# Two transformer blocks on one core: the recurrence's gates as three products of rounded parts

## The chip, the cores and the metric

The kernel runs on one core of a Trainium2 chip. A core has a matrix engine (TensorE, PE in the profile, with its weight loads as PEld), three engines for elementwise work (VectorE or DVE, ScalarE or ACT, GpSimd or POOL), a synchronisation engine whose queue starts transfers (SP), an on-chip memory of 128 partitions (SBUF) and an accumulator memory of eight banks (PSUM). The engines run their own instruction streams and wait for one another by semaphores. The metric is the device time of one execution in microseconds, smaller being better.

## The reference

Two transformer blocks follow each other on one sequence of 256 tokens with 1024 features, all in f32. The change concerns one part of the first block, the gated recurrence over 1344 channels:

```python
def rg_lru(x, w_a, b_a, w_x, b_x, lam):
    xb = x.reshape(bsz, s, RNN_BLOCKS, RNN_BLOCK_W)        # 16 blocks of 84 channels
    r = sigmoid(einsum('bsnc,ncd->bsnd', xb, w_a).reshape(bsz, s, D_RNN) + b_a)
    i = sigmoid(einsum('bsnc,ncd->bsnd', xb, w_x).reshape(bsz, s, D_RNN) + b_x)
    log_a = LRU_C * r * log_sigmoid(lam)
    a = exp(log_a)
    u = sqrt(-expm1(2.0 * log_a)) * (i * x)
    # h[t] = a[t] * h[t-1] + u[t]

hr = rg_lru(causal_dwconv(rx, rnn_conv_w, rnn_conv_b), ...)
y_rnn = (hr * gelu(rgate)) @ w_rnn_out
```

Around it stand the input projection, an attention with compressed, selected and windowed branches, the output projections, a gated feed-forward part with a short convolution, and a second block of attention, spatial gating and feed-forward.

## The kernel before

All weights are one stream of chunks, at most 128 x 2048 numbers each, in the order of `CHUNKS` (lines 91 to 131). A product in f32 would cost PE several passes, so a chunk is split into two parts that PE takes in one pass each: ACT copies the chunk from its arrival slot `RAW` into `WH` with rounding (line 629), and DVE writes the rest, raw minus rounded, into `WL` (line 1074). Activations are split in the same way (`AH` and `AL`, `BH` and `BL`, and so on), and a product is the sum of high x high, high x low and low x high (lines 1735, 1736 and 1740 for the projections of the recurrence).

There are two arrival slots in this stage (`NRAW`), and three places for split chunks (`NSLOT`). While PE works on chunk c, ACT and DVE split chunk c + 2. SP starts the load of a chunk when the slot's previous chunk has had its low part taken (line 538).

The recurrence runs in five groups of 2, 3, 2, 2 and 2 tiles of up to 126 channels, interleaved with the chunks of the merge gates ("mg"). In the order of the chunks it goes: `rnn` chunks (a projection for one tile of channels and its output gate), `mg` chunks, and behind each group one small chunk `ri` with the weights of the two gates for the group. What each engine does for chunk c is its "window". For an `rnn` chunk PE projects one tile; ACT evicts it into `XC` with the first convolution tap and into `RGT` (lines 793 and 795); DVE adds the other three taps (line 1298). The `ri` chunk is the only one here that isn't split: its f32 weights are loaded straight into the place of the chunk (`WF`, line 551), when the chunk that was there is done, and PE multiplies them in f32 with `XC` (line 2065). Each tile takes one bank for both gates. A block of 84 channels does not fit whole into the tiles, so one block per group is split over the first two tiles, 42 channels each, and its cross terms are small products with 42 rows and 42 columns (lines 2073 and 2075), one of each pair in the lower half of the array's rows and one in the upper half. The gates share two banks with the neighbouring projections (`mb_bank`, line 1828), so a product waits until the reader of two uses earlier has evicted its bank.

After the gates, ACT evicts them as TR and TI (lines 806 and 807), DVE and ACT form a, u and the scan over several windows (`rg_group` says in which), and ACT and DVE split the result into `AH` and `AL` for the projection `ro` (lines 656 and 1153).

The attention of the first block runs through the same windows as twelve units: PE forms scores (line 1858), DVE the maxima (lines 1095 and 1097), ACT the exponentials with their sums (`unit_exp`, line 650), DVE scales them (line 1112), PE transposes them (line 1869) and multiplies by the values (line 1892). The scores of a unit wait for the exponentials of the unit before (line 1852). ACT's order inside a window is written out by hand (lines 1036 to 1056): split a chunk, the exponentials of a unit, the evictions of the chunk, and the small steps of the window. POOL computes only reciprocal roots for the norms (line 575), and some steps of the second block; in the recurrence it has no work.

Of the kernel before, what the change touches and what calls it, by code (L numbers as in the profile page):

```python
# [33 lines left out]
RP = 126  # L34
# [36 lines left out]
def gate_cols(g):  # L71

    return RG_TILES[g] * RP + HB
# [41 lines left out]


def ffn_order(up, n, down, lag=5):

    out, d = [], 0
    for i in range(n):  # L120
        out.append((up, i, CHUNK, True))
        if i >= 2 * d + lag:
# [13 lines left out]
               max(RNN_NO[i] for i in range(RG_AT[g], RG_AT[g + 1])) + 1 for g in range(NG)]  # L136
SPLIT_NO = [sum(1 for x in CHUNKS[:c] if x[3]) for c in range(NCH)]
# [6 lines left out]
def arrival_slots():  # L144

    last, uses, out = [None] * (NRAW + 3), [0] * (NRAW + 3), {}
    for c, (kind, i, _, is_split) in enumerate(CHUNKS):
        if not is_split:
            continue
        third = kind in ("wo", "up", "dn") or kind == "ro" and i >= 1 or kind == "in2" and i < 3  # L150
        slots = list(range(NRAW)) + [NRAW] * third + [NRAW + 1] * (kind in ("up2", "dn2"))
        slots += [NRAW + 2] * (kind == "kv")
        slot = min(slots, key=lambda n: -1 if last[n] is None else last[n])
        out[c] = (slot, last[slot], uses[slot])
        last[slot] = SPLIT_NO[c]
        uses[slot] += 1
    return out
# [87 lines left out]
def two_block_program(nc, A_w, A_x, A_cols, A_consts, A_g1, A_g2, A_og, A_gln, A_ln1, A_ln2, A_ws, A_out):  # L245
    ctx = ExitStack()
    with ctx:
# [45 lines left out]
        def const(name):  # L293
# [160 lines left out]
        y_mean, y_std, eps_ready, x0_low, y_ln, xt4_done, xt4_hi, xt4_lo, up2_silu, up2_prod = (sem(n) for n in (  # L454
            "y_mean", "y_std", "eps_ready", "x0_low", "y_ln", "xt4_done", "xt4_hi", "xt4_lo", "up2_silu", "up2_prod"))
        up2_hi, up2_lo, z_gain, wt_ready, rnn_in, xw_ready, gate_t_done, x_sq2 = (sem(n) for n in (
            "up2_hi", "up2_lo", "z_gain", "wt_ready", "rnn_in", "xw_ready", "gate_t_done", "x_sq2"))
        half_copied, halves_summed = sem("half_copied"), sem("halves_summed")
# [101 lines left out]
        def _(eng):  # L560
# [32 lines left out]
            power(crs[0:NKV * CP, :], css[0:NKV * CP, :], 1, HD, EPS, kc_rstd)  # L593
            for t in range(NT):
# [18 lines left out]
        def _(eng):  # L613
# [358 lines left out]
            def half_copy(c, n, bank):  # L972

                eng.wait_ge(chunk_done, c + 1)
                if n >= 4:
                    eng.wait_ge(up_conv if n - 4 < N_UP else up2_prod, n - 3 if n - 4 < N_UP else n - 3 - N_UP)
# [23 lines left out]
            def up2_silu_of(i):  # L1000
                eng.wait_ge(halves_summed, N_UP + i + 1)
                if i >= 4:
                    eng.wait_ge(up2_lo, i - 3)
                eng.activation(SG[:, i % 4, :], HLS[:, i % 4, 0, :], ACT.Silu).then_inc(up2_silu, 1)

            def up2_first(i):
                eng.wait_ge(up2_prod, i + 1)
                if i >= NA:
                    eng.wait_ge(chunk_done, AT["dn2", (i - NA) // 2] + 1)
                eng.activation(AH[:, i % NA, :], SG[:, i % 4, :], ACT.Copy).then_inc(up2_hi, 1)  # L1010
# [25 lines left out]
            for c in range(NCH):  # L1036
# [6 lines left out]
                if c == SPLIT_AHEAD:  # L1043
                    split(c + 2)
                u = unit_at(c - W0)
# [14 lines left out]
        def _(eng):  # L1060
# [7 lines left out]
            def split(c):  # L1068

                if c >= NCH or not CHUNKS[c][3]:  # L1070
# [445 lines left out]
            def up2_product(i):  # L1516
                eng.wait_ge(halves_summed, N_UP + i + 1)
                eng.wait_ge(up2_silu, i + 1)
                eng.tensor_tensor(SG[:, i % 4, :], HLS[:, i % 4, 1, :], SG[:, i % 4, :], ALU.mult)\
                   .then_inc(up2_prod, 1)  # L1520

            def up2_second(i):
                eng.wait_ge(up2_hi, i + 1)
                eng.tensor_tensor(AL[:, i % NA, :], SG[:, i % 4, :], f32(AH[:, i % NA, :]), ALU.subtract)\
                   .then_inc(up2_lo, 1)
# [188 lines left out]
        def _(eng):  # L1714
# [15 lines left out]
            def f_tile(out, c, col0, m, H, L, nk=KD, parts=P):  # L1730
# [6 lines left out]
                eng.wait_ge(w_lo, SPLIT_NO[c] + 1)  # L1737
# [5 lines left out]
            def hl_tile(bank, c, col0, HL):  # L1743
# [5 lines left out]
                eng.wait_ge(w_lo, SPLIT_NO[c] + 1)  # L1749
# [36 lines left out]
            def tile1_pass(bank, c, HL, lo_ready):  # L1786
# [3 lines left out]
                eng.wait_ge(w_lo, SPLIT_NO[c] + 1)  # L1790
# [4 lines left out]
            def t_part(out, c, cols, ks, H, L, t, start, stop):  # L1795
# [7 lines left out]
                eng.wait_ge(w_lo, SPLIT_NO[c] + 1)  # L1803
# [195 lines left out]
            def main(c):  # L1999
# [58 lines left out]
                if kind == "ri":  # L2058
                    eng.wait_ge(mb_dve, RNN_THROUGH[i])
                    w = plain(c).rearrange("p (a n) -> p a n", a=2)  # L2060
                    banks = {}
                    for m, t in enumerate(gate_order(i)):
                        banks[t] = mb_bank(MB_NO[c] + m)
                        for which in range(2):
                            last = eng.matmul(PS[0:RP, banks[t], 256 * which:256 * which + 256],  # L2065
                                              w[0:RP, which, RP * t:RP * t + RP], XC[:, i % 2, t, :], start=(which == 0),
                                              stop=(t == 2), skip_group_check=True)
                        if t == 2:
                            last.then_inc(ri_part, 1)
                    for which in range(2):  # L2070
                        cols = slice(256 * which, 256 * which + 256)
                        other = w[:, which, RP * RG_TILES[i]:gate_cols(i)]
                        ins = eng.matmul(PS[64:64 + HB, banks[0], cols], other[0:HB], XC[0:HB, i % 2, 1, :],
                                         start=False, stop=(which == 1), skip_group_check=True)
                        last = eng.matmul(PS[0:HB, banks[1], cols], other[64:64 + HB], XC[64:64 + HB, i % 2, 0, :],
                                          start=False, stop=(which == 1), skip_group_check=True)
                    ins.then_inc(ri_part, 1)
                if kind == "ao":
# [10 lines left out]
                    for ks in parts:  # L2089
# [7 lines left out]
                        eng.wait_ge(w_lo, SPLIT_NO[c] + 1)  # L2097
# [4 lines left out]
                if kind == "ro":  # L2102
# [14 lines left out]
                    eng.wait_ge(w_lo, SPLIT_NO[c] + 1)  # L2117
# [34 lines left out]
                if kind in ("dn", "dn2"):  # L2152
                    first_bank, lo_s, n_all = (2, up_lo, N_UP // 2) if kind == "dn" else (0, up2_lo, N_UP2 // 2)
# [6 lines left out]
                    eng.wait_ge(lo_s, 2 * i + 2)  # L2160
# [4 lines left out]
                    elif i == n_all - 2:  # L2165
# [6 lines left out]
                        eng.wait_ge(lo_s, 2 * i + 3)  # L2172
                        eng.wait_ge(up_hi if kind == "dn" else up2_hi, 2 * i + 4)
# [11 lines left out]
                        eng.wait_ge(w_lo, SPLIT_NO[c + 1] + 1)  # L2185
# [3 lines left out]
                        eng.wait_ge(lo_s, 2 * i + 4)  # L2189
# [331 lines left out]
```

## Time and profile before

| | |
|---|---|
| Median of 3 runs | 812.28 us (812.08 to 812.28) |
| Span of the profiled execution, first to last instruction | 810.6 us |
| PE busy | 799.6 us (99%) |
| DVE busy | 599.4 us (74%) |
| ACT busy | 487.0 us (60%) |
| POOL busy | 27.1 us (3%), 38 instructions |
| Chain that ended last | PE 93%, ACT 3%, DVE 2% |

The span is the time from the first to the last instruction of one profiled execution; the runs' times hold a little more around it. Busy times are sums over instructions. Matmuls are pipelined, so one of them is shown with a longer duration than the distance to the next; distances between starts are what a stream of them costs. The chain follows the last instruction back, at each step to what released it. A wait is shown as idle time in brackets behind the instruction that waited, with the one that released it. A matmul in f32 shows as two passes.

### The profile page before, as it was taken

The page shows a single profiled execution, that of the slowest core. Times are in us where ns is not written, and L with a number is a line of the kernel's source. Part 1 is how long each engine was busy: PE and PEld are TensorE (multiplying, and loading weights), DVE is VectorE, ACT ScalarE, POOL GpSimd, SP SyncE. Part 2 cuts the span into 40 slices and gives each one's busy share as a digit, 9 for nine tenths or more (in the row PEclk, how much of TensorE's full clock was granted, in tenths as well). Part 3 has the DMA queues.
Part 4 walks back from the last instruction along what each step waited for, and adds up shares of the span by engine and source line. Part 5 has one row for each costly group of instructions (what it writes and reads, how often), then busy time and mean ns, then how long its engine had stood idle before and what let it go on. Part 6 is the DMA issues. An engine that isn't in the chain of part 4 may idle for free.

```text
span 810.6 us, 11913 instructions
## 1 busy us (share of the span) xinstructions
PE 799.6 (99%) x4813; PEld 693.2 (86%) x4813; DVE 599.4 (74%) x773; ACT 487.0 (60%) x738; POOL 27.1 (3%) x38
## 2 busy tenths in 40 slices
PE   8999999999999999999999999999999999999996
PEld 7889998888888888988888888888888988888885
DVE  6774698998957986897878778877777665655556
ACT  6555598877757454765666566546755654544552
POOL 1102000000000000000000000020110000000000
PEclk9999999999999999999999999999999999999999
DMA  8446432342434674456455555764453655555441
GB/s 337 164 156 251 170 126 104 118 155 73 151 119 159 229 288 156 156 188 227 160 206 174 201 197 175 256 237 147 146 196 121 211 201 196 174 219 191 161 152 52
DMA packets 22630, 143.79 MB, mean 177 GB/s; under 512 B 2608, under 2 KB 3248, under 8 KB 8240
## 3 DMA queue, kind: packets, MB, share of 16 engines
q1 hardware_dynamic: 20880, 137.72, 48.3%
q10 hardware_dynamic: 1696, 5.31, 1.8%
q8 instruction: 38, 0.62, 0.3%
q14 instruction: 16, 0.13, 0.0%
HBM read 141.97 MB, written 1.05 MB: 176 GB/s over the span
## 4 chain that ended last, share of the span: by engine, by line
PE 93%; ACT 3%; DVE 2%; DMA 1%; issue 1%; DVEq 0%; SPq 0%; ACTq 0%
PE PS L1748 19%; PE PS L1752 10%; PE PS L1801 10%; PE PS L1802 10%; PE PS L1805 10%; PE PS L1735 5%; PE PS L1736 4%; PE PS L1740 4%; PE PS L2115 3%; PE PS L1764 2%; PE PS L2094 2%; PE PS L1858 1%; PE PS L1892 1%; PE PS L2119 1%; PE PS L1869 1%; PE PS L2065 1%
## 5 line engine op out<-in xcount | busy, mean ns | idle before, releaser
L1074 DVE TENSOR_TENSOR WL<-RAW,WH 128x2048 fp32r<-128x2048 f32 (+2 forms) x127 | 285.1, 2247 | 31.1 <-ACT WH L629 31.0
L629 ACT ACTIVATE WH<-RAW 128x2048 fp32r<-128x2048 f32 (+2 forms) x127 | 238.2, 1877 | 47.0 <-PE PS L1805 25.7
L1490 DVE TENSOR_TENSOR HLS<-PS,HLS 128x512 f32<-128x512 f32 x46 | 31.7, 689 | 92.7 <-ACT HLS L977 92.7
L1748 PE MATMUL PS<-CHL,WH 128*128 128x512 f32 x352 | 87.9, 392 | 0.0
L1735 PE MATMUL PS<-BHL,WH 128*126 128x256 f32 (+1 forms) x336 | 83.6, 287 | 0.0
L977 ACT ACTIVATE HLS<-PS 128x512 f32<-128x512 f32 x46 | 27.4, 595 | 90.7 <-PE PS L1752 86.3
L1736 PE MATMUL PS<-BHL,WH 128*126 128x256 f32 (+1 forms) x336 | 81.8, 282 | 0.0
L1748 PE MATMUL PS<-BHL,WH 128*128 128x512 f32 x320 | 79.9, 392 | 0.0
L1748 PEld LDWEIGHTS PS<-CHL,WH 128*128 128x128 f32 x352 | 63.9, 189 | 11.8
L1802 PE MATMUL PS<-WH,AHL 128*128 128x512 f32 x176 | 68.8, 391 | 0.0
L1801 PE MATMUL PS<-WH,AHL 128*128 128x512 f32 x176 | 68.7, 390 | 0.0
L1735 PEld LDWEIGHTS PS<-BHL,WH 128*126 128x126 f32 (+1 forms) x336 | 63.4, 189 | 4.6 <-issue 3.7
L1748 PEld LDWEIGHTS PS<-BHL,WH 128*128 128x128 f32 x320 | 58.1, 189 | 10.7
L1736 PEld LDWEIGHTS PS<-BHL,WH 128*126 128x126 f32 (+1 forms) x336 | 63.5, 189 | 0.0
L1801 PE MATMUL PS<-WH,BHL 128*128 128x512 f32 x160 | 63.2, 395 | 0.0
L1802 PE MATMUL PS<-WH,BHL 128*128 128x512 f32 x160 | 62.3, 390 | 0.0
L1805 PE MATMUL PS<-WL,AHL 128*128 128x512 f32 x176 | 54.4, 390 | 0.0
L1752 PEld LDWEIGHTS PS<-CHL,WL 128*128 128x128 f32 x352 | 48.0, 190 | 3.4
L1752 PE MATMUL PS<-CHL,WL 128*128 128x256 f32 x352 | 49.1, 282 | 0.0
L1740 PE MATMUL PS<-BHL,WL 128*126 128x256 f32 (+1 forms) x336 | 46.7, 281 | 0.0
L1752 PEld LDWEIGHTS PS<-BHL,WL 128*128 128x128 f32 x320 | 43.7, 190 | 3.1
L1501 DVE SCALAR_TENSOR_TENSOR CG<-HLS,CV,CG 128x255 f32<-128x255 f32 (+1 forms) x96 | 44.2, 481 | 1.7
(313 smaller groups left out, 1311.1 us busy)
## 6 DMA issues: line engine op xcount, KB each, us to landing
RAW<-in_w_stream SPq DMA_DIRECT2D x108, 1024.0 KB, 4.8
RAW<-in_w_stream SPq DMA_DIRECT2D x11, 1008.0 KB, 4.9
RAW<-in_w_stream SPq DMA_DIRECT2D x8, 704.0 KB, 4.5
WF<-in_w_stream SPq DMA_DIRECT2D x2, 1024.0 KB, 5.4
LN<-in_ln ACTq DMA_DIRECT2D x2, 1024.0 KB, 5.2
WF<-in_w_stream SPq DMA_DIRECT2D x4, 294.0 KB, 3.6
X<-in_x SPq DMA_DIRECT2D x2, 512.0 KB, 4.2
RAW<-in_w_stream SPq DMA_DIRECT2D x2, 512.0 KB, 6.8
```

The lines of the kernel that those rows point to most:

```text
L629: eng.activation(WH[:, c % NSLOT, 0:CHUNKS[c][2]], raw(c), ACT.Copy).then_inc(w_hi, 1)
L1074: eng.tensor_tensor(WL[:, c % NSLOT, 0:CHUNKS[c][2]], raw(c), f32(WH[:, c % NSLOT, 0:CHUNKS[c][2]]), ALU.subtract).then_inc(w_lo, 1)
L1490: eng.tensor_tensor(HLS[:, n % 4, :, :], PS[:, bank:bank + 2, 0:TOK], HLS[:, n % 4, :, :], ALU.add)\
L1501: ins = eng.scalar_tensor_tensor(o, HLS[:, i % 4, v, 0:TOK - s], col("fw", (2 - s) * 2 * N_UP + f), o, ALU.mult, ALU.add)
L1735: eng.matmul(out, wh, H[0:parts, k, :], start=(k == 0), stop=False)
L1736: eng.matmul(out, wh, L[0:parts, k, :], start=False, stop=False)
L1740: last = eng.matmul(out, wl, H[0:parts, k, :], start=False, stop=(k == nk - 1))
L1748: eng.matmul(PS[:, bank, :], wh, HL[:, k, :, :].rearrange("p a t -> p (a t)"), start=(k == 0), stop=False)
L1752: last = eng.matmul(PS[:, bank, 0:TOK], wl, HL[:, k, 0, :], start=False, stop=(k == KD - 1))
L1801: eng.matmul(out, H[:, k, tile], wh, start=(start and n == 0), stop=False)
L1802: eng.matmul(out, L[:, k, tile], wh, start=False, stop=False)
L1805: last = eng.matmul(out, H[:, k, tile], WL[:, s, lo_:lo_ + cols], start=False, stop=(stop and n == len(ks) - 1))
```

## The change

The gate chunks `ri` become split chunks like the others: they arrive in `RAW`, ACT rounds them into `WH`, and POOL, not DVE, takes the low part into `WL`. The tiles of channels are split too: ACT rounds each tile of `XC` into `AH` after DVE's taps, in the window behind its projection, ahead of the exponentials of that window, and POOL takes the low part into `AL`. PE then computes the gates as three products of rounded parts each. The small products of the split block write 106 output rows (0 to 105) instead of 42 at their own offset, with weights padded by zeros, so a gate chunk grows by 64 columns per gate (from 588 to 716 columns for a group of two tiles, from 840 to 968 for three). Counting of the low parts is divided: `LOW_NO` counts those of DVE, `RG_LOW_NO` those of POOL. The semaphores of the second feed-forward part (`up2_silu`, `up2_prod`, `up2_hi`, `up2_lo`) are replaced by going on counting in those of the first (`up_gelu`, `up_prod`, `up_hi`, `up_lo`), with the same events. Every wait on `w_lo` by `SPLIT_NO[c] + 1` becomes one by `LOW_NO[c] + 1`; these lines are left out below.

```diff
 def gate_cols(g):
-    return RG_TILES[g] * RP + HB
+    return RG_TILES[g] * RP + 64 + HB
...
-        out += [("ri", g, 2 * gate_cols(g), False)]
+        out += [("ri", g, 2 * gate_cols(g), True)]
...
+LOW_NO = [sum(1 for x in CHUNKS[:c] if x[3] and x[0] != "ri") for c in range(NCH)]
+_low_order = []
+for _c in range(NCH):
+    _low_order += [x[:2] for x in CHUNKS[_c + 2:_c + 3] if x[0] == "ri"]
+    _low_order += [x[:2] for x in CHUNKS[max(0, _c - 1):_c] if x[0] == "rnn"]
+RG_LOW_NO = {_k: _n + 1 for _n, _k in enumerate(_low_order)}
...
@@ SP, loads
                     if before is not None:
-                        eng.wait_ge(w_lo, before + 1)
+                        if CHUNKS[before][0] == "ri":
+                            eng.wait_ge(rg_low, RG_LOW_NO[CHUNKS[before][:2]])
+                        else:
+                            eng.wait_ge(w_lo, LOW_NO[before] + 1)
...
@@ POOL, behind the roots of the first block's norms
+            for c in range(NCH):
+                if c + 2 < NCH and CHUNKS[c + 2][0] == "ri":
+                    s, n = (c + 2) % NSLOT, CHUNKS[c + 2][2]
+                    eng.wait_ge(w_hi, SPLIT_NO[c + 2] + 1)
+                    eng.tensor_tensor(WL[:, s, 0:n], raw(c + 2), f32(WH[:, s, 0:n]), ALU.subtract).then_inc(rg_low, 1)
+                if c and CHUNKS[c - 1][0] == "rnn":
+                    i = CHUNKS[c - 1][1]
+                    G, t = RG_OF[i]
+                    eng.wait_ge(xc_hi, RNN_NO[i] + 1)
+                    eng.tensor_tensor(AL[0:RP, i, :], XC[:, G % 2, t, :], f32(AH[0:RP, i, :]), ALU.subtract).then_inc(rg_low, 1)
...
@@ ACT
+            def rg_round(i):
+                G, t = RG_OF[i]
+                eng.wait_ge(mb_dve, RNN_NO[i] + 1)
+                eng.activation(AH[0:RP, i, :], XC[:, G % 2, t, :], ACT.Copy).then_inc(xc_hi, 1)
...
                 if c == SPLIT_AHEAD:
                     split(c + 2)
+                if c and CHUNKS[c - 1][0] == "rnn":
+                    rg_round(CHUNKS[c - 1][1])
                 u = unit_at(c - W0)
                 if u is not None:
                     unit_exp(u)
...
@@ DVE
             def split(c):
-                if c >= NCH or not CHUNKS[c][3]:
+                if c >= NCH or not CHUNKS[c][3] or CHUNKS[c][0] == "ri":
                     return
...
@@ PE
                 if kind == "ri":
-                    eng.wait_ge(mb_dve, RNN_THROUGH[i])
-                    w = plain(c).rearrange("p (a n) -> p a n", a=2)
+                    eng.wait_ge(rg_low, max(RG_LOW_NO["rnn", k] for k in range(RG_AT[i], RG_AT[i + 1])))
+                    wh, wl = (W[:, c % NSLOT, 0:2 * gate_cols(i)].rearrange("p (a n) -> p a n", a=2) for W in (WH, WL))
                     banks = {}
                     for m, t in enumerate(gate_order(i)):
+                        k = RG_AT[i] + t
                         banks[t] = mb_bank(MB_NO[c] + m)
+                        outs = [PS[0:RP, banks[t], 256 * which:256 * which + 256] for which in range(2)]
                         for which in range(2):
-                            last = eng.matmul(PS[0:RP, banks[t], 256 * which:256 * which + 256],
-                                              w[0:RP, which, RP * t:RP * t + RP], XC[:, i % 2, t, :], start=(which == 0),
+                            rows = wh[0:RP, which, RP * t:RP * t + RP]
+                            eng.matmul(outs[which], rows, AH[0:RP, k, :], start=(which == 0), stop=False, skip_group_check=True)
+                            eng.matmul(outs[which], rows, AL[0:RP, k, :], start=False, stop=False, skip_group_check=True)
+                        for which in range(2):
+                            last = eng.matmul(outs[which], wl[0:RP, which, RP * t:RP * t + RP], AH[0:RP, k, :], start=False,
                                               stop=(t == 2), skip_group_check=True)
                         if t == 2:
                             last.then_inc(ri_part, 1)
+                    first = RG_AT[i]
                     for which in range(2):
                         cols = slice(256 * which, 256 * which + 256)
-                        other = w[:, which, RP * RG_TILES[i]:gate_cols(i)]
-                        ins = eng.matmul(PS[64:64 + HB, banks[0], cols], other[0:HB], XC[0:HB, i % 2, 1, :],
-                                         start=False, stop=(which == 1), skip_group_check=True)
-                        last = eng.matmul(PS[0:HB, banks[1], cols], other[64:64 + HB], XC[64:64 + HB, i % 2, 0, :],
-                                          start=False, stop=(which == 1), skip_group_check=True)
+                        for n, (W, A) in enumerate(((wh, AH), (wh, AL), (wl, AH))):
+                            other = W[:, which, RP * RG_TILES[i]:gate_cols(i)]
+                            ins = eng.matmul(PS[0:64 + HB, banks[0], cols], other[0:HB, 0:64 + HB], A[0:HB, first + 1, :],
+                                             start=False, stop=(which == 1 and n == 2), skip_group_check=True)
+                            last = eng.matmul(PS[0:64 + HB, banks[1], cols], other[64:64 + HB, 0:64 + HB], A[64:64 + HB, first, :],
+                                              start=False, stop=(which == 1 and n == 2), skip_group_check=True)
                     ins.then_inc(ri_part, 1)
```

## Rows read from the trace of the kernel before

**Rows 1.** The page: span, busy time of each engine, chain by engine.
```profile
span 810.6 us, 11913 instructions
...
PE 799.6 (99%) x4813; PEld 693.2 (86%) x4813; DVE 599.4 (74%) x773; ACT 487.0 (60%) x738; POOL 27.1 (3%) x38
...
PE 93%; ACT 3%; DVE 2%; DMA 1%; issue 1%; DVEq 0%; SPq 0%; ACTq 0%
```
**Rows 2.** Windows: length, busy PE, PEld, DVE, ACT, POOL, clock, DMA.
```profile
98.80:122.50 23.70, 23.70 (x191) 21.69 (x190) 22.57 (x33) 22.77 (x48) 0.00 (x0) 1.00 0.41 147
...
137.30:152.90 15.60, 15.08 (x126) 13.82 (x126) 14.82 (x18) 14.82 (x36) 0.00 (x0) 1.00 0.52 194
...
200.00:243.00 43.00, 43.00 (x339) 36.29 (x337) 32.44 (x43) 27.62 (x54) 0.00 (x0) 1.00 0.38 130
```
**Rows 3.** Line 2065, the gates' f32 products: passes, duration in ns, shape.
```profile
L2065 PE MATMUL PS<-XC,WF x44: 377/379/482, 98.9 to 240.7; 126*126 126x256 f32 x44
```
**Rows 4.** The chain through the gates of group 2: start, length, engine, line.
```profile
161.83 1.92 PE PS L2065 x8
163.75 0.34 PE PS L2073
...
164.77 1.06 PE PS L1869 x8
```
**Rows 5.** Timeline of PE, a projection in rounded parts: start, length.
```profile
103.01 0.28 PE L1736 MATMUL PS<-BHL,WH 128*126 128x256 f32 x1
...
104.66 0.28 PE L1736 MATMUL PS<-BHL,WH 128*126 128x256 f32 x1
```
**Rows 6.** Line 1858, one unit's scores: passes, first and last start.
```profile
L1858 PE MATMUL PS<-KT,QT x8: 376/376/480, 114.7 to 115.5; 64*128 64x256 f32 x8
```
**Rows 7.** The chain through the gates of group 1.
```profile
123.61 0.47 ACT TR L806
...
124.50 1.13 PE PS L2065 x4
...
126.62 0.64 PE PS L1884 x4
```
**Rows 8.** Timeline of ACT ahead of group 1's gates.
```profile
117.35 1.93 ACT L629 ACTIVATE WH<-RAW 128x2048 fp32r<-128x2048 f32 x1
...
122.41 0.61 ACT L800 ACTIVATE MG<-PS 128x512 f32<-128x512 f32 x1
```
**Rows 9.** The chain from the scores of one unit to those two units on.
```profile
136.16 1.09 PE PS L1858 x8
...
149.58 1.28 ACT L650
...
152.86 1.13 PE PS L1858 x8
```
**Rows 10.** Waits from 80 to 245 us: total, times, longest.
```profile
PEld PS L1858 <- ACT SMC L650: 0.8, 1, 0.8
```
**Rows 11.** Timeline of all engines at the scores behind unit 8.
```profile
192.30 0.30 PEld L1858 LDWEIGHTS PS<-KT,QT 64*128 64x128 f32 x4 [0.17 <-ACT SM L650]
```
**Rows 12.** Groups of ACT's roundings by shape: count, busy us, mean ns, idle before.
```profile
L629 ACT ACTIVATE WH<-RAW 128x1408 fp32r<-128x1408 f32 x8 | 10.9, 1374 | 4.5 <-DMA RAW<-in_w_stream 3.7 <-PE PS L2119 0.5 <-PE PS L2100 0.3
...
L668 ACT ACTIVATE CHL<-PS 128x256 fp32r<-128x256 f32 x8 | 3.1, 391 | 2.0 <-PE PS L1892 2.0
```
**Rows 13.** Timeline at the second block's rotation, where POOL adds two tiles.
```profile
533.03 2.29 DVE L1074 TENSOR_TENSOR WL<-RAW,WH 128x2048 fp32r<-128x2048 f32 x1 [2.79 <-ACT WH L629]
...
536.66 2.55 POOL L600 TENSOR_TENSOR RQK<-RT 128x512 f32<-128x512 f32 x2 [214.64 <-DVE RT L1388]
...
538.31 3.06 DVE L1074 TENSOR_TENSOR WL<-RAW,WH 128x2048 fp32r<-128x2048 f32 x1 [0.47 <-ACT WH L629]
```
**Rows 14.** Timeline of DVE, the low part that frees the arrival slot.
```profile
110.39 2.28 DVE L1074 TENSOR_TENSOR WL<-RAW,WH 128x2048 fp32r<-128x2048 f32 x1
```
**Rows 15.** Transfers by line: count, size of one, us from issue to landing.
```profile
RAW<-in_w_stream SPq DMA_DIRECT2D x108, 1024.0 KB, 4.8
```

More of the change, by code:

```diff
@@ L154, in arrival_slots @@
         out[c] = (slot, last[slot], uses[slot])
-        last[slot] = SPLIT_NO[c]
+        last[slot] = c
         uses[slot] += 1
@@ L453, in two_block_program @@
             "mix_done", "os_ready", "os_ss", "os_rstd", "mr_ready", "mrt_done", "mrt_hi", "mrt_lo"))
[L454 to L458, printed above, removed]
+        y_mean, y_std, eps_ready, x0_low, y_ln, xt4_done, xt4_hi, xt4_lo = (sem(n) for n in (
+            "y_mean", "y_std", "eps_ready", "x0_low", "y_ln", "xt4_done", "xt4_hi", "xt4_lo"))
+        z_gain, wt_ready, rnn_in, xw_ready, gate_t_done, x_sq2 = (sem(n) for n in (
+            "z_gain", "wt_ready", "rnn_in", "xw_ready", "gate_t_done", "x_sq2"))
+        half_copied, halves_summed, xc_hi, rg_low = (sem(n) for n in ("half_copied", "halves_summed", "xc_hi", "rg_low"))
         def wait_tile(eng, c, t):
@@ L975, in half_copy @@
                 if n >= 4:
-                    eng.wait_ge(up_conv if n - 4 < N_UP else up2_prod, n - 3 if n - 4 < N_UP else n - 3 - N_UP)
+                    eng.wait_ge(up_conv if n - 4 < N_UP else up_prod, n - 3)
                 eng.activation(HLS[:, n % 4, :, :], PS[:, bank:bank + 2, TOK:2 * TOK], ACT.Copy).then_inc(half_copied, 1)
@@ L1002, in up2_silu_of @@
                 if i >= 4:
-                    eng.wait_ge(up2_lo, i - 3)
-                eng.activation(SG[:, i % 4, :], HLS[:, i % 4, 0, :], ACT.Silu).then_inc(up2_silu, 1)
+                    eng.wait_ge(up_lo, N_UP + i - 3)
+                eng.activation(SG[:, i % 4, :], HLS[:, i % 4, 0, :], ACT.Silu).then_inc(up_gelu, 1)
             def up2_first(i):
-                eng.wait_ge(up2_prod, i + 1)
+                eng.wait_ge(up_prod, N_UP + i + 1)
                 if i >= NA:
                     eng.wait_ge(chunk_done, AT["dn2", (i - NA) // 2] + 1)
-                eng.activation(AH[:, i % NA, :], SG[:, i % 4, :], ACT.Copy).then_inc(up2_hi, 1)
+                eng.activation(AH[:, i % NA, :], SG[:, i % 4, :], ACT.Copy).then_inc(up_hi, 1)
             def gained_hi(kp):
@@ L2116, in main @@
                                    start=(k == 0), stop=False)
-                    eng.wait_ge(w_lo, SPLIT_NO[c] + 1)
+                    eng.wait_ge(w_lo, LOW_NO[c] + 1)
                     for k in range(NR):
@@ L2152, in main @@
                 if kind in ("dn", "dn2"):
-                    first_bank, lo_s, n_all = (2, up_lo, N_UP // 2) if kind == "dn" else (0, up2_lo, N_UP2 // 2)
+                    first_bank, before, n_all = (2, 0, N_UP // 2) if kind == "dn" else (0, N_UP, N_UP2 // 2)
                     def down_half(cc, j, t, n):
@@ L2158, in down_half @@
                                       j == 0, j == n_all - 1)
-                    eng.wait_ge(lo_s, 2 * i + 2)
+                    eng.wait_ge(up_lo, before + 2 * i + 2)
                     if i < n_all - 2:
@@ L2171, in main @@
                         eng.wait_ge(w_hi, SPLIT_NO[c + 1] + 1)
-                        eng.wait_ge(lo_s, 2 * i + 3)
-                        eng.wait_ge(up_hi if kind == "dn" else up2_hi, 2 * i + 4)
+                        eng.wait_ge(up_lo, before + 2 * i + 3)
+                        eng.wait_ge(up_hi, before + 2 * i + 4)
                         s = (c + 1) % NSLOT
@@ L2188, in main @@
                             eng.matmul(outs[n], AH[:, units[1], 0:P], weights(WL, 1, n), start=False, stop=False)
-                        eng.wait_ge(lo_s, 2 * i + 4)
+                        eng.wait_ge(up_lo, before + 2 * i + 4)
                         for n in range(2):
@@ L2414, in gates_blocks @@
             first, second = rows_of[0, 64:64 + HB], rows_of[1, 0:HB]
-            out[0:HB, which, n * RP:] = dense[second[:, None], first[None, :]]
-            out[64:64 + HB, which, n * RP:] = dense[first[:, None], second[None, :]]
+            out[0:HB, which, n * RP + 64:] = dense[second[:, None], first[None, :]]
+            out[64:64 + HB, which, n * RP:n * RP + HB] = dense[first[:, None], second[None, :]]
         return out.reshape(P, -1)
```

20 lines of the change are left out of this document (10 added, 10 removed).

## The prediction

> **What bounds the kernel now.** I read the page first: PE is busy 99% of the span and holds 93% of the chain that ended last [rows 1]. So a microsecond that TensorE saves is one saved, as long as nobody makes PE wait in its place. The change lies in the recurrence, some 85 to 243 us. Next I cut that stretch into windows [rows 2]: from 98.80 to 122.50 ACT is busy 22.77 of 23.70 us and DVE 22.57; from 137.30 to 152.90 both are busy 14.82 of 15.60; from 200 to 243 ACT has 15.4 us free. The granted clock is 1.00 (2.4 GHz), so no clock is to be gained. The reader is to see that in the first half three engines run side by side without slack, and that the change gives work to one of them (ACT) and to a neighbour of another (POOL beside DVE), to take some from PE. Then I asked the chain, the timelines and the waits where PE already waits for ACT. There are three such places: the gates of group 1, where the chain leaves PE for ACT's TR at 123.61 [rows 7]; the scores at 152.86, where the chain runs 15.6 us through DVE and ACT before it comes back to PE and PE's weight load idles 0.8 us [rows 9, 10]; and the scores at 192.30, which wait 0.17 us for ACT's exponentials [rows 11].
>
> **PE: the gate products.** A plain f32 product of 126x126 by 256 columns shows as two passes; 44 passes are 22 products [rows 3]. A pass goes by every 0.216 us: eight of them and a change of the array's shape hold 1.92 us of the chain in group 2 [rows 4], and 8 x 0.216 = 1.73. A product of rounded parts is one pass of 0.118: between the starts at 103.01 and 104.66 lie 14 of them [rows 5], 1.65/14. Three of them are 0.354 against 0.432. A group of two tiles has four such products: 1.73 us now, 12 x 0.118 = 1.42 after.
>
> The small products over the split blocks (L2073 and L2075, two pairs in a group) run side by side now: from 163.75 to 164.77 four double passes and a second change of shape go by [rows 4], 4 x 0.216 = 0.86 us and 0.16. After, a group has six pairs, and each product writes 106 output rows instead of 42, so both of a pair lie in the same columns of the array. The scores (L1858) show that two products in different halves of the rows with all 128 columns still run together: eight f32 passes start within 114.7 to 115.5 [rows 6]; one behind another, 7 x 0.216 = 1.5 us would lie between the first start and the last. Bounds for six pairs: side by side 6 x 0.118 = 0.71, in sequence 12 x 0.118 = 1.42. I take 0.71, L1858 being the nearest row. The two changes of shape (0.35 us of the 2.94 from 161.83 to 164.77 [rows 4]) stay.
>
> Group of two tiles: 1.73 + 0.86 - 1.42 - 0.71 = 0.46 us saved. Group 1 with three tiles: 12 x 0.216 + 0.86 - 18 x 0.118 - 0.71 = 0.62, if nothing waits. All five: 4 x 0.46 + 0.62 = 2.5 us of PE. In sequence instead it is 5 x 0.71 = 3.5 us more, a loss of 1.0.
>
> **ACT: what it gets.** Five roundings of gate weights (716 columns, 968 for group 1) and eleven of a channel tile (256 columns). Nearest rows: 1408 columns 1.374 us, 256 columns 0.391 [rows 12]; on the line between them 716 columns take 0.78 and 968 some 1.0. Successive ACT instructions overlap by about 0.1, so on a full engine I take 0.7, 0.9 and 0.3 (bounds 0.6 to 0.8, 0.8 to 1.0, 0.25 to 0.39). Where ACT waits for PE or DVE anyway this is hidden: the weights of groups 0 and 4 and tiles 4, 0, 1, 6, 8, 9, 10; where that cover is gone each costs its price. Not hidden are three places.
>
> (a) Ahead of the gates of group 1 ACT works almost without a gap, from the rounding at 117.35 to the eviction of MG at 122.41 and on [rows 8]. This group needs two banks for three tiles: its second tile needs MG evicted, its third needs TR and TI of the first. New in this row are the weights of group 1 (0.9) and tiles 2 and 3 (0.3 each), less the 0.46 that group 0 gave: +1.04 at MG. A gap of 0.3 ahead of TR closes, so the third tile starts 0.75 late, at 125.25 instead of 124.50 [rows 7]. From there to 126.62 it took 2.12 us, now 0.31 less: 127.06. PE is 0.44 behind the kernel before. Group 0 had put it 0.46 ahead, so this place costs 0.90.
>
> (b) The chain of 136.16 to 152.86. DVE takes the maxima when PE has the scores; ACT exponentiates, rounds weights, evicts, loads two tables, and near 149.58 a third for the next exponentials, which PE awaits at 152.86 [rows 9]. The weights of group 2 and tile 5 are now rounded just ahead of that table load: 0.7 + 0.3. PE idles there already [rows 10], so all of it arrives: +1.0.
>
> (c) The same order comes again with unit 8: weights of group 3 and tile 7 stand ahead of the exponentials for which PE waits 0.17 [rows 11]. +1.0.
>
> Groups 2, 3 and 4 give 0.46 each. Sum: -0.46 + 0.90 + 1.0 - 0.46 + 1.0 - 0.46 - 0.46 = +1.06 us.
>
> **POOL, the new wait, and the loads.** PE now waits, ahead of a group, for POOL's low parts: 16 new subtractions. Nearest row: two additions of 512 columns in 2.55 us, 1.3 each [rows 13]. 256 columns: between 0 and 1.3, taken as 0.7; 716 and 968 columns: between 1.3 and, in proportion, 1.8 or 2.45, taken at the upper end. Group 1 is tightest: tile 3 is rounded behind the weights of 117.35, to about 120.2 by the new clock; POOL ends at 121.0; PE comes at 122.0. So 1.0 us of cover; the other groups have the window of a whole chunk. Behind POOL's wait stand its own later subtractions and nothing else before the second norm. Behind ACT's wait for DVE's taps stand the exponentials; in each window the taps end before the rounding ahead of it does, so it costs nothing, and if DVE is late by more, that excess.
> The gate weights now come through the two arrival slots instead of straight into their place, and a chunk behind them loads one slot later. Tightest is the chunk rounded at 117.35: its slot is freed by the low part of 110.39 + 2.28 = 112.67 [rows 14], 112.2 after, and a load takes 4.8 [rows 15]: 117.0 against a need at 118.1. Free; if late, by the excess alone. SP's four waits for PE ahead of these loads go; nobody was waiting for them. The renamed semaphores of the later stages wait for the same events: nothing.
>
> **Total.** The profiled execution has 810.6 us of span and the runs a median of 812.28; the 1.7 us around the span stay. 810.6 + 1.06 + 1.7 = 813.3 us.
>
> **Rivals.**
> *The extra work on ACT is absorbed*: all of PE's 2.5 us stay. For: ACT's free time from 200 on [rows 2]. Against: three places where PE waits for ACT already. 812.3 - 2.5 = 809.8 us.
> *POOL keeps DVE out* (slower). POOL's additions at 536.66 lie partly over a rounding by DVE at 538.31 that takes 3.06 us, where the same one at 533.03 took 2.29 [rows 13]: 0.77 lost to one overlap. The place is 98.80 to 152.90, where DVE is nearly as full as PE: weights of groups 1 and 2 and tiles 2, 3 and 5 are 2.45 + 1.8 + 3 x 0.7 = 6.4 us of POOL. If half of it falls on DVE operations with two inputs in SBUF (roundings, scalings, scans) and delays the maxima, +3.2: 816.5 us. It decides from the point where over 0.6 us of it stands ahead of the maxima in (b), or POOL ends tile 3 over 1.0 us late. Against: by my timing DVE reads PSUM there (taps, maxima) while POOL works.
> The Trainium skill, SBUF — State Buffer, section "SBUF: two separate sides", says that the port pair which the two share is a lock held for a whole instruction, and that the loser blocks fully. The 0.77 us agree. By that rule alone all of POOL's some 17 us could come on top; the row bears out the mechanism, not that each one collides.
> *The small pairs run in sequence* (slower): 3.5 us more than the forecast, 816.8 us. For: their columns now overlap, which L2073 and L2075 never did. Against: L1858 [rows 6].
>
> **Chances.** Forecast 0.53 (own range 812.0 to 814.5: ACT's costs at both bounds, and place (a) between 0.3 and 1.2); absorbed 0.15; POOL's port 0.20; pairs in sequence 0.12. What can't be told from no change is 0.2%, 1.6 us: 810.7 to 813.9. Faster: most of the absorbed case and a little of the forecast, 0.16. Slower: nearly all of the two slow rivals and the upper end of the forecast, 0.37. Same: 0.47. Range 810.2 to 816.5: it leaves out the better half of the absorbed case and the worse half of the slow ones.
>
> **What would show it.** Gate passes 0.118 apart, the small ones starting in pairs (or singly); ACT's new roundings right ahead of the table loads near 150 and 190, and PE's idle time before the scores there about 1 us longer each than 0.8 and 0.17; PE waiting for MG's eviction inside group 1. The forecast is wrong if PE's idle time in the recurrence doesn't grow by some 3 us, if DVE's roundings there last over 2.5 us, or if PE waits for POOL ahead of the gates.

## The result, and the profile after

The changed kernel takes 814.46 us against 812.28 before, both medians: +2.2 us, a ratio of 1.0027; the ratio of the means is 1.0038 (95% interval 1.0024 to 1.0052). Forecast were 813.3 us, +1.06, in a range of 810.2 to 816.5. So it is a little slower, by slightly more than the 0.2% that a measurement of this kernel can tell from no change, and the forecast had the sign right and half the size. (Of the changed kernel and of three kernels of the experiments, late_round, after_side and no_pool, 11 of 33 executions took 3 to 5 us more than the others, at a granted clock of 0.991 to 0.995 instead of 0.997 to 0.999, and of the other kernels none did; the ratios with an interval are ratios of means and count them, so the text below goes by the medians, and by that of the other three executions for no_pool.)

The page after, against [rows 1]: the span and the busy time of TensorE (PE) and the others, then the chain by engine.

```profile
span 812.4 us, 12034 instructions
...
PE 798.2 (98%) x4855; PEld 695.8 (86%) x4855; DVE 602.3 (74%) x773; ACT 494.0 (61%) x754; POOL 49.6 (6%) x54
...
PE 89%; ACT 6%; DVE 3%; issue 1%; DMA 1%; SPq 0%; DVEq 0%; ACTq 0%
```

The reader is to see two things that pull apart. PE is busy 1.4 us less than before, so the three products do save PE time. But the span is 1.8 us longer: PE idles 3.2 us more, and the chain now lies with ScalarE (ACT) for 6% of the span instead of 3%. VectorE (DVE) works as many instructions as before and is busy 2.9 us longer.

The gates themselves, one line of the small products and the end of group 2 on PE's timeline; they answer to [rows 3, 4]:

```profile
L2106 PE MATMUL PS<-AHL,WH x20: 275/277/367, 100.9 to 243.8; 42*106 42x256 f32 x20
```

```profile
165.63 0.28 PE L2106 MATMUL PS<-AHL,WH 42*106 42x256 f32 x1
165.63 0.28 PE L2108 MATMUL PS<-AHL,WH 42*106 42x256 f32 x1
165.75 0.28 PE L2106 MATMUL PS<-AHL,WL 42*106 42x256 f32 x1
165.75 0.28 PE L2108 MATMUL PS<-AHL,WL 42*106 42x256 f32 x1
```

Both products of a pair start together, and pairs follow 0.12 us apart, though both write all 106 rows: they run side by side, in sequence they would be twice as long. Where PE waits, from the waits of 80 to 245 us (in total, times, longest), against [rows 10, 11]:

```profile
PE PS L1884 <- ACT SMC L669: 1.5, 1, 1.5
...
PE PS L2094 <- ACT MG L824: 1.2, 1, 1.2
...
PE PS L1884 <- ACT SM L669: 0.8, 1, 0.8
...
PE PS L1895 <- DVE PT L1145: 0.5, 1, 0.5
```

By place: MG's eviction inside the gates of group 1 (new), a copy of DVE behind the gates of group 2 (new), and the scores of places (b) and (c): 1.5 and 0.8 us, where PE's weight loads waited 0.8 and 0.17 before and wait 1.7 and 1.1 now. The chain of the changed kernel shows what stands in front of each of the three that wait for ACT; (a) first, against [rows 7, 8]:

```profile
116.23 1.00 ACT WH L648
117.23 0.31 ACT AHL L680
...
120.56 0.30 ACT AHL L680
...
124.11 0.49 ACT MG L824
...
125.86 0.38 PE PS L2094
...
150.63 0.69 ACT WH L648
151.32 0.30 ACT AHL L680
...
151.64 1.28 ACT L669
...
155.33 0.28 ACT RGT L819
...
190.96 0.69 ACT WH L648
191.66 0.30 ACT AHL L680
...
191.98 1.28 ACT L669
```

The lines L648 and L680 in this list are the new roundings: 1.0 for the weights of group 1, 0.69 for those of the others, 0.30 for a tile. At (b) and (c) they stand right ahead of the load of the table for the exponentials (L669 with no tile beside it), as [rows 9] led one to expect; at (a) they stand among ACT's other work, all of it ahead of MG's eviction at 124.11.

**How far PE is behind, place by place.** This table is read from the timelines: each row is one PE instruction of the kernel before, by its start; the columns say how much later the same instruction starts in the other kernels' profiles (minus is earlier). The experiments' columns are explained below.

```
start   what stands there          after  act_   pool_  pe_    late_  no_    after_ f32_12
before                                    only   only   only   round  pool   side
 91.34  before any gate            +0.46  +0.04  -0.18  -0.15  +0.25  +0.16  -0.06  -0.01
101.72  behind group 0             -0.06  +0.04  -0.19  -0.67  -0.26  -0.37  -0.57  -0.53
121.67  ahead of group 1           +0.01  +0.04  +0.80  -0.61  -0.19  -0.31  -0.50  -0.46
126.55  behind group 1, place (a)  +1.09  +1.31  +1.72  -1.00  +0.89  +0.81  +0.59  -0.46
152.86  scores, place (b)          +2.06  +2.29  +2.26  -1.01  +0.89  +1.81  +0.58  -0.47
164.77  behind group 2             +2.07  +2.29  +2.27  -1.00  +1.89  +1.81  +0.64  -0.46
192.30  scores, place (c)          +2.96  +3.16  +2.28  -0.99  +1.91  +2.71  +0.65  -0.45
204.57  behind group 3             +2.53  +3.15  +2.27  -1.41  +2.13  +2.30  +0.22  -0.88
242.04  behind group 4             +2.10  +3.16  +2.28  -1.83  +1.68  +1.89  -0.21  -1.30
317.59  well behind the recurrence +2.07  +3.27  +2.37  -1.77  +1.64  +2.33  -0.18  -0.94
```

The first column says where the time went: 0.46 before anything of the change has run, -0.52 in group 0, +1.15 from there through group 1, +0.97 at (b), nothing in group 2, +0.89 at (c), -0.43 each in groups 3 and 4. The first of these is the landing of the first weights, and it differs from profile to profile (first row): it belongs to an execution, not to the change. Without it the recurrence costs 1.64 us.

### The profile page after: what moved, and what is told of

Same layout as the page of the kernel before. It is cut to its first block, busy times and chain, and to the rows that moved or that the text cites. A ratio compares the mean times of both kernels' runs of the same rounds, so it can differ in the third digit from the quotient of the medians.

```text
span 812.4 us, 12034 instructions
## 1 busy us (share of the span) xinstructions
PE 798.2 (98%) x4855; PEld 695.8 (86%) x4855; DVE 602.3 (74%) x773; ACT 494.0 (61%) x754; POOL 49.6 (6%) x54
## 4 chain that ended last, share of the span: by engine, by line
PE 89%; ACT 6%; DVE 3%; issue 1%; DMA 1%; SPq 0%; DVEq 0%; ACTq 0%
PE PS L1774 19%; PE PS L1778 10%; PE PS L1827 10%; PE PS L1828 10%; PE PS L1831 10%; PE PS L1761 4%; PE PS L1762 4%; PE PS L1766 4%; PE PS L2148 3%; PE PS L1790 2%; PE PS L2127 2%; PE PS L2152 1%; PE PS L1918 1%; ACT WH L648 1%; PE PS L1798 1%
## 5 line engine op out<-in xcount | busy, mean ns | idle before, releaser
L648 ACT ACTIVATE WH<-RAW 128x2048 fp32r<-128x2048 f32 (+3 forms) x132 | 242.3, 1838 | 48.6 <-PE PS L1831 26.2
```

The costliest lines, as they stand in the source:

```text
L648: eng.activation(WH[:, c % NSLOT, 0:CHUNKS[c][2]], raw(c), ACT.Copy).then_inc(w_hi, 1)
```

## The experiments

The theory: ACT's roundings in front of three things that PE waits for cost what the recurrence lost, GpSimd (POOL) next to nothing, and PE's products save what was worked out. The rival: POOL's subtractions, which keep DVE out, are the payer. The expectations speak of the scores at (b) and (c) as those of units 5 and 8. The first four kernels take the change apart or move one piece of it.

**ACT's part alone** (act_only): the roundings are added to the kernel before, at the same places of ACT's program.

```diff
 # kernel before, ScalarE
+def rg_round(i):
+    eng.wait_ge(mb_dve, RNN_NO[i] + 1)
+    eng.activation(<unread 126x256>, XC[:, G % 2, t, :], ACT.Copy)
+def ri_round(c):                       # 716 or 968 columns
+    eng.wait_ge(chunk_done, c - NSLOT + 1)
+    eng.activation(<unread>, f32(BHL ...), ACT.Copy)
...
                     split(c + 2)
+                    ri_round(c + 2)
...
+                if c and CHUNKS[c - 1][0] == "rnn":
+                    rg_round(CHUNKS[c - 1][1])
                 u = unit_at(c - W0)
```

> The kernel before with ScalarE's additional roundings alone: the same sizes (716 or 968 columns for a gate chunk, 256 for a tile) at the same places of its program, written to buffers that nobody reads; TensorE keeps its float32 gates and GpSimd does nothing new. Theory (ScalarE's roundings ahead of the exponentials are what costs): TensorE is set back at three places, 1.4 to 1.8 us ahead of the gates of group 1, 1.0 at the scores of unit 5, 0.9 at the scores of unit 8, and nothing is given back, so +3.3 to +3.7 us against before, 815.6 to 816.0. Rival (GpSimd's hold on the port is the payer and ScalarE's work is absorbed): within 0.3 us of before, 812.0 to 812.6. The 0.47 us by which the first weight load came late in the trace after should be absent here if it belongs to the changed weight stream, present or absent if it is chance.

815.51 us, +3.2; ratio 1.0039 (1.0026 to 1.0052). In the table +1.27 at (a), +0.98 at (b), +0.87 at (c), nothing elsewhere: the theory's three places, with (a), and so the time, 0.1 under its lower bound. PE's waits are those of the changed kernel:

```profile
PE PS L1874 <- ACT SMC L650: 1.5, 1, 1.5
...
PE PS L2081 <- ACT MG L812: 1.0, 1, 1.0
...
PE PS L1874 <- ACT SM L650: 0.8, 1, 0.8
```

So ACT's part suffices for all three setbacks. That does not yet say that POOL's part does nothing.

**POOL's part alone** (pool_only).

```diff
 # kernel before, GpSimd, ahead of the second norm
+for c in range(NCH):
+    if c + 2 < NCH and CHUNKS[c + 2][0] == "ri":
+        eng.wait_ge(chunk_done, c)
+        eng.tensor_tensor(<unread, 716 or 968 columns>, BHL, BHL, ALU.subtract)
+    if c and CHUNKS[c - 1][0] == "rnn":
+        eng.wait_ge(mb_dve, RNN_NO[i] + 1)
+        eng.tensor_tensor(<unread 126x256>, BH, BL, ALU.subtract)
```

> The kernel before with GpSimd's subtractions alone: 716 or 968 columns for each gate chunk and 256 for each tile of channels, released by the chunk before and by VectorE's finished tile, on operands that do not change, into buffers that nobody reads. Theory: the port is shared but what it holds up is off the path, so 0 to +0.3 us, 812.2 to 812.6, though single VectorE instructions show up at twice their length beside a GpSimd one. Rival (the port is the payer of the difference of 2.2 us): +1.0 to +2.2 us, 813.3 to 814.5.

(The subtractions are written to a part of `AL` that is in use later, so ACT also waits for them ahead of its rounding of a group's result; the trace shows no idle time of ACT from that.)

814.91 us, +2.6; ratio 1.0031 (1.0019 to 1.0043): the theory's number is wrong by 2.3 us, and the rival's is passed. The place is plain on the timelines of POOL and DVE:

```profile
108.62 2.42 POOL L608 TENSOR_TENSOR AHL<-BHL 128x968 fp32r<-128x968 f32 x1 [14.08 <-PE PS L1762]
```

```profile
108.47 0.42 DVE L1655 TENSOR_TENSOR SC<-SC,CN 128x256 f32<-128x256 f32 x1
108.93 2.39 DVE L1656 TENSOR_TENSOR SC<-SC,crw 128x256 f32<-128x256 f32 x1
111.36 0.43 DVE L1655 TENSOR_TENSOR SC<-SC,CN 128x256 f32<-128x256 f32 x1
```

The same operation on 256 columns takes 0.42 us ahead of the subtraction and 2.39 beside it: it ends 0.3 us behind it. DVE is then 2 us behind its own times, and PE pays 0.99 ahead of group 1, 0.92 at (a) and 0.54 at (b). POOL alone is nearly as dear as ACT alone. Here its subtractions come earlier than in the changed kernel (the one of group 1 at 108.62 against 117.31), since nothing has to be rounded first; what POOL costs with the changed kernel's releases but without ACT's work was not tried.

**PE's part alone** (pe_only): the products of the changed kernel on parts that exist from the start.

```diff
 # kernel before, TensorE
-    last = eng.matmul(outs, w[0:RP, which, ...], XC[:, i % 2, t, :], ...)      # f32
+    eng.matmul(outs[which], BH[0:RP, ...], BH[0:RP, t, :], ...)
+    eng.matmul(outs[which], BH[0:RP, ...], BL[0:RP, t, :], ...)
+    last = eng.matmul(outs[which], BL[0:RP, ...], BH[0:RP, t, :], ...)
...
+    # and the small pairs likewise, six of 42x106 in place of two of 42x42 in f32
```

> The kernel before with TensorE's three products alone: the gates' matmuls take weights and channels from the rounded parts of the normalized input, which are there from the start, so no rounding and no subtraction is added; the gates' values are not those of the reference, the order and sizes of the matmuls are those of the changed kernel. Theory: 0.46 us saved in each two-tile group and 0.62 in group 1, of which group 2's may be lost to VectorE's chain behind it as in the trace after: -2.0 to -2.5 us, 809.8 to 810.3. Rival (the three-product gates save only what the trace after shows at three groups, because TensorE waits elsewhere for the same end): -1.2 to -1.5 us, 810.8 to 811.1.

810.55 us, -1.8; ratio 0.9978 (0.9970 to 0.9987): between the two. Group 0 gives 0.52 and groups 3 and 4 0.42 each, as worked out; group 1 gives 0.39 of 0.62 (PE waits 0.23 there for ACT's TI) and group 2 nothing. Behind group 2 PE is done early and waits for what it did not wait for before:

```profile
163.77 1.06 PE L1869 MATMUL PS<-CN,SMC 128*128 128x128 f32 x8 [0.46 <-DVE PT L1119]
```

0.46 is the whole of group 2's saving. In the kernel before DVE's copy of PT and PE's last gate product end together, so nobody saw that DVE's chain was as long: no wait stood there.

**The roundings behind the exponentials** (late_round).

```diff
 # changed kernel, ScalarE; late(c): c + 2 is a gate chunk and c has a unit
-                    split(c + 2)
+                    if not late(c):
+                        split(c + 2)
...
-                if c and CHUNKS[c - 1][0] == "rnn":
+                if c and CHUNKS[c - 1][0] == "rnn" and not late(c):
                     rg_round(CHUNKS[c - 1][1])
...
                 if u is not None:
                     unit_exp(u)
+                if late(c):
+                    split(c + 2)
+                    rg_round(CHUNKS[c - 1][1])
                 ...
                 side(c)
```

> The changed kernel with one thing moved: where an exponential step follows directly (units 4 and 8), ScalarE rounds the gate chunk and the tile of channels behind the exponentials instead of ahead of them. Theory: the setbacks of 0.97 and 0.90 us at the scores of units 5 and 8 go, group 1's stays: 812.6 us, and 812.1 if group 2's saving of 0.46 comes back with them. Rival (the setbacks come from VectorE held by GpSimd, or ScalarE's later work of the same stretch is late instead): 814.1 to 814.8, as the changed kernel.

814.33 us, +2.0; ratio 1.0039 (1.0025 to 1.0054): no better than the changed kernel, so the time goes by the rival. But the table says that the theory's step happened: nothing is lost at (b) or (c) any more. It is lost later: +1.00 behind group 2, and group 3, which gave 0.43, costs 0.22. Two waits, PE's behind group 2 and DVE's start of the chain that sets it:

```profile
PE PS L1902 <- DVE PT L1152: 1.5, 1, 1.5
```

```profile
155.52 1.52 DVE L1331 SCALAR_TENSOR_TENSOR XC<-PS,CV,XC 126x255 f32<-126x255 f32 x3 [2.05 <-ACT RGT L822]
156.95 0.68 DVE L1152 COPY PT<-PS 128x512 f32<-128x512 f32 x1
```

DVE's taps wait 2.05 us for ACT's eviction of the projection (L822); from there DVE works without a gap, taps, maxima, scaling, low part, scan, to the copy of PT that PE wants behind group 2. The eviction stands in side(c), and I had put 1.0 us of rounding in front of it. That is the chain of pe_only, met from the other end.

**Also behind the evictions** (after_side), **and no subtractions** (no_pool).

```diff
 # after_side: the same two calls one line further down
                 side(c)
+                if late(c):
+                    split(c + 2)
+                    rg_round(CHUNKS[c - 1][1])
```

```diff
 # no_pool: changed kernel, GpSimd
-for c in range(NCH):
-    ... both subtractions
 # TensorE: the low operands are BL in place of AL and WL
-    eng.wait_ge(rg_low, ...)
+    eng.wait_ge(xc_hi, RNN_THROUGH[i])
```

> The changed kernel with the gate chunk's and the first tile's rounding at units 4 and 8 behind the exponentials and also behind the evictions of that stretch's projection, which VectorE's taps wait for. Theory: the run before gave its 0.97 and 0.90 us back because VectorE, whose chain from the taps to the copy of the probabilities sets the end there, got the projection 1.0 us late; now it does not, so both are gained: 812.4 to 812.7 us, with group 1's setback left. Rival (any 1.0 us of ScalarE's in this stretch is paid once, wherever it stands): 814.1 to 814.6.

812.68 us, +0.4 against +2.2 for the changed kernel (ratio 1.0013, 1.0003 to 1.0022): 1.8 us gained by moving two calls, as the theory had it. In the table (b), group 2 and (c) cost -0.01, 0.06 and 0.01. ACT evicts first and rounds then, and PE waits at (b) no longer than in the kernel before:

```profile
153.71 0.40 ACT L822 ACTIVATE RGT<-PS 126x256 f32<-126x256 f32 x1
153.98 0.82 ACT L648 ACTIVATE WH<-RAW 128x716 fp32r<-128x716 f32 x1
154.67 0.44 ACT L683 ACTIVATE AHL<-XC 126x256 fp32r<-126x256 f32 x1
```

```profile
PE PS L1891 <- ACT SMC L669: 0.5, 1, 0.5
PE PS L1902 <- DVE PT L1152: 0.5, 1, 0.5
```

The second of these waits is again group 2's saving that goes to DVE.

> The changed kernel without GpSimd's subtractions: ScalarE rounds gates and channels as there and TensorE does the three products, but it takes the low parts from those of the normalized input, which are there from the start (the gates' low products are not those of the reference). Theory: no difference to the changed kernel, 814.2 to 814.6 us, since the 1.43 and 1.53 us by which a subtraction held VectorE at 151.55 and 191.79 lie beside ScalarE's longer way to the same exponentials. Rival (the setbacks at the scores of units 5 and 8 belong to those two holds): one or both go, 812.5 to 813.6.

814.30 us, +2.0, the median of three executions (814.09 to 814.53), ratio 1.0044 (1.0030 to 1.0058): as the changed kernel, though on few executions. The table's steps are those of the changed kernel to 0.04 us up to place (c), and from the first row to the one behind group 4 it loses 1.73 us against 1.64. So in the recurrence of the changed kernel the subtractions cost nothing. That the two totals agree as well is in part chance: here PE waits 0.38 us more for DVE's merge well behind the recurrence (below), and the time around the span is 0.25 us shorter (see the rest of +2.2, further down). That the subtractions do hold DVE there is seen on the changed kernel's own timelines, POOL's and DVE's:

```profile
151.40 1.72 POOL L607 TENSOR_TENSOR WL<-RAW,WH 128x716 fp32r<-128x716 f32 x1 [29.73 <-ACT WH L648]
```

```profile
151.55 2.65 DVE L1138 TENSOR_TENSOR SM<-SM,wt 128x1024 f32<-128x1024 f32 x1
154.13 1.47 DVE L1165 TENSOR_TENSOR XC<-XC,TI 126x768 f32<-126x768 f32 x1
155.70 1.52 DVE L1324 SCALAR_TENSOR_TENSOR XC<-PS,CV,XC 126x255 f32<-126x255 f32 x3
```

The scaling L1138 takes 2.65 us where it took 1.22 before, and L1165 behind it, beside the next subtraction, 1.47 where it took 0.95. But the taps at 155.70 could not have started sooner: ACT's eviction for them (L819 in the chain above) ended at 155.61, behind its roundings. At (c) L1165 alone is held, 2.22 us where it took 0.69:

```profile
191.79 2.22 DVE L1165 TENSOR_TENSOR XC<-XC,TI 126x512 f32<-126x512 f32 x1
```

Two late chains meet at one point, and only the later one is paid.

**The best of both** (f32_12): groups 1 and 2, where the change gained nothing, stay in float32, and the roundings of group 3 go behind the evictions.

```diff
+F32_GROUPS = (1, 2)
-        out += [("ri", g, 2 * gate_cols(g), True)]
+        out += [("ri", g, 2 * gate_cols(g), g not in F32_GROUPS)]
...
 def rg_round(i):
     G, t = RG_OF[i]
+    if G in F32_GROUPS:
+        return
...
+                if kind == "ri" and i in F32_GROUPS:
+                    ... the float32 products of the kernel before
```

> Groups 0, 3 and 4 as three products with the rounding behind the evictions, groups 1 and 2 in float32 as in the kernel before (no rounding and no subtraction for them). Theory: no setback at the gates of group 1 or at the scores of unit 5; of group 0's saving 0.2 us is left (TensorE then waits for the same eviction as before), and 0.43 each of groups 3 and 4: 1.1 us under before, 810.9 to 811.6. Rival (group 3's rounding costs at unit 8 or behind it what group 3 saves): 811.7 to 812.3, no difference to before.

811.51 us, 0.8 under before: ratio 0.9990 (0.9981 to 0.9999), within the range of the theory. It is the fastest of the three whole kernels, but against the one before by half of what this measurement can well tell. Groups 0, 3 and 4 keep 0.45, 0.43 and 0.42 on PE, group 0 more than expected. Then 0.36 is given back between 242 and 318 us, where PE waits for DVE's merge:

```profile
PE PS L2181 <- DVE MG L1361: 0.5, 1, 0.5
```

That wait is 0.2 us in the profiles of act_only, pool_only and pe_only, 0.4 in that of no_pool and absent in those of the changed kernel, late_round and after_side. What sets it was not followed up.

## Why the prediction was right or wrong

The sign and the three places were right; the size was half of what was measured. None of the signs that would have spoken against the forecast came: PE's idle time from 80 to 245 us grows by 3.8 us (0.6 to 4.4), DVE's roundings there stay under 2.3 us, and PE waits for POOL nowhere.

**PE's saving per group**: right. 0.46 was worked out for two tiles; the runs show 0.52, 0.43 and 0.43 (groups 0, 3, 4), the pairs side by side. That refutes the rival of pairs in sequence.

**"Groups 2, 3 and 4 give 0.46 each"**: this is the step that failed, for group 2. It was counted as saved because PE showed no wait behind it [rows 4]. pe_only, with no other work added, shows that group 2's products lie beside a chain of DVE that ends at the same time, so shortening them gives nothing. That is 0.46 of the 0.58 us by which the sum of the recurrence (1.06 forecast, 1.64 seen) was short. The gap could have been seen in the profile before: DVE's timeline there is without a gap from the taps at 153.64 to the copy that ends at 164.62, and PE's next instruction starts at 164.77 [rows 4]. "No wait" meant "no slack on either side". The first and the last line of that stretch of the kernel before:

```profile
153.64 1.52 DVE L1298 SCALAR_TENSOR_TENSOR XC<-PS,CV,XC 126x255 f32<-126x255 f32 x3 [1.06 <-ACT RGT L795]
...
163.94 0.68 DVE L1119 COPY PT<-PS 128x512 f32<-128x512 f32 x1
```

**Place (a), 0.90**: right in mechanism, 0.25 too small. MG's eviction and the third tile are what PE waits for, as forecast. The third tile was to be 0.75 late and, with the 0.46 of the start taken off, is 0.90 late (125.86 against 124.50), since the gap ahead of TR that was to close is 0.11 us of idle time and not 0.3 (TR starts at 123.61, the eviction ahead of it ends at 123.50); the products behind it then give 0.27 instead of 0.31, and the lead from group 0, which this place costs as well, was 0.52 instead of 0.46.

**Places (b) and (c), 1.0 each**: right: 0.97 and 0.89, and act_only gives the same with nothing else changed.

**POOL costs nothing**: right for the recurrence of the changed kernel (no_pool), but by luck. The argument was that DVE reads PSUM while POOL works. In two places it does not, DVE is held 1.95 us at (b) and 1.53 at (c), and what hides this is that ACT is late by as much or more at the same points. Alone, and with earlier releases, the subtractions cost 2.6 us, so the rival that POOL keeps DVE out had its mechanism right, with a price (3.2 us) of the size that they cost there.

**The loads, the new wait for low parts, the semaphores**: nothing in the recurrence, as forecast. ACT does wait 1.52 us for the load of the first gate chunk, at 88.63, which it did not before, but group 0 has its whole saving behind it.

**The rest of +2.2.** The recurrence gives 1.64. The 0.46 at the start is in this one profile; four profiles of kernels with a changed weight stream have between -0.06 and +0.25 there, so it can't be put down to the change. The medians differ by 2.18. Of the remaining 0.5, a quarter of a microsecond lies where the forecast had a term that "stays", the 1.7 us around the span: the time of an execution less its span is 2.00 us in the mean of the changed kernel's seven executions (1.95 to 2.05) and 1.75 in those of the kernel before that were measured beside the experiments (1.69 to 1.81). It is 1.98 in late_round, 1.99 in after_side and 1.93 in f32_12, but 1.74 to 1.78 in act_only, pool_only, pe_only and no_pool. So it comes with the kernels in which PE waits for POOL's subtractions; what it consists of no run shows. Where the last 0.3 us is stays open.

**The rival that the extra work is absorbed**: false as it stands, but after_side shows what it lacked. The work on ACT can be absorbed at (b) and (c); it has to stand behind what others wait for, and not only behind the exponentials.

## What to carry to other kernels

Where two engines reach a point together, the profile shows a wait for neither, and a saving on one of them was worth nothing here: before counting one, follow the other engine's timeline back from the first instruction behind it. Work that is added to an in-order engine belongs behind all that others wait for in that stretch, so list each reader of what the engine makes next; after one reader was served first (late_round), the next one was late by the same 1.0 us. And costs of parts measured alone don't add: +3.2, +2.6 (with POOL's work released earlier) and -1.8 make +4.0, the whole is +2.2. The time around the span is a term to measure too, and not a constant: here it grew by 0.25 us, and by 0.18 in f32_12, which gained 0.8 in all.

## What the runs showed of the hardware

A subtraction on POOL of 256, 716 or 968 columns takes 0.73, 1.72 and 2.30 us where nothing disturbs it. A DVE operation with both inputs in SBUF that starts while one runs ends only behind it (2.39 us in place of 0.42 in pool_only); the Trainium skill, SBUF — State Buffer, section "SBUF: two separate sides", states such a lock for a whole instruction, and this row agrees. It works the other way too: in the changed kernel a subtraction of 256 columns that starts beside DVE's low part of 2016 columns (95.34 to 97.60) shows 2.51 us.

```profile
95.69 2.51 POOL L612 TENSOR_TENSOR AHL<-XC,AHL 126x256 fp32r<-126x256 f32 x1 [3.76 <-ACT AHL L680]
```

DVE operations that read PSUM were not held: in late_round a subtraction of 716 columns starts at 154.46 and one of 256 at 156.15, and the taps beside them (155.52 above) take 1.52 us as before.

```profile
154.46 1.73 POOL L607 TENSOR_TENSOR WL<-RAW,WH 128x716 fp32r<-128x716 f32 x1 [32.98 <-ACT WH L648]
156.15 0.74 POOL L612 TENSOR_TENSOR AHL<-XC,AHL 126x256 fp32r<-126x256 f32 x1
```
